# Five column sums of squares taken by TensorE as two fp32r products of the total's head and rest, two of them asked for one or two groups later

## The reference, cut to what matters

```python
h = rmsnorm(x, g_mix)
z = h @ w_in                                   # lx, lg, q, k, v
y_lru = rmsnorm(rg_lru(conv(lx)) * gelu(lg), g_lru_out)
y_att = rmsnorm(chunk_window_attention(q, k, v, sinks), g_attn_out)
x = x + concatenate([y_lru, y_att]) @ w_out
h = rmsnorm(x, g_ffn)
x = x + square(relu(h @ w_ff1)) @ w_ff2
gate = sigmoid(rmsnorm(x, g_ple) @ w_ple_gate)
x = x + gate * (p @ w_ple_proj)
return rmsnorm(x, g_final)
```

## Time and profile before

| | us |
|---|---|
| median of 3 runs | 1088.73 |
| lowest and highest of the 3 | 1082.97 and 1088.93 |
| the profiled execution, whole | 1087.07 |
| its span, first to last instruction | 1085.3 |

### The profile page before, as it was taken

The page is one execution under the profiler, slowest core; times in us unless marked ns, Lnnn a source line. Parts: engine busy times, 40 slices in busy tenths (PEclk is TensorE's granted clock), DMA queues, the critical chain, the costliest instruction groups (busy, mean ns, idle before and its releaser), DMA issues.

```text
span 1085.3 us, 13820 instructions
## 1 busy us (share of the span) xinstructions
PE 1068.8 (98%) x4930; PEld 877.6 (81%) x4930; DVE 688.1 (63%) x928; ACT 460.3 (42%) x797; POOL 423.8 (39%) x285
## 2 busy tenths in 40 slices
PE   9999999999998999999999999999999999999996
PEld 7888787777876788888888888888888888888896
DVE  7997778878699644544544544544545545697558
ACT  7446745555584322422422422422422422565334
POOL 0121151334127235445445445445445345294221
PEclk9999999999999999999999999999999999999998
DMA  8111102111011112112112112112112111420004
GB/s 330 40 40 39 39 1 88 39 40 40 1 40 39 39 39 77 39 39 77 39 39 77 39 39 77 39 39 77 39 39 76 40 39 73 160 78 1 1 1 156
DMA packets 20162, 61.05 MB, mean 56 GB/s; under 512 B 2080, under 2 KB 4128, under 8 KB 20128
## 3 DMA queue, kind: packets, MB, share of 16 engines
q1 hardware_dynamic: 19440, 59.82, 15.1%
q10 hardware_dynamic: 688, 0.79, 0.2%
HBM read 56.40 MB, written 4.19 MB: 56 GB/s over the span
## 4 chain that ended last, share of the span: by engine, by line
PE 79%; DVE 6%; ACT 2%; issue 1%; DVEq 0%; ACTq 0%
PE bank L576 25%; PE bank L577 25%; PE bank L578 25%; PE bank L683 1%; DVE xT L1781 1%; PE bank L713 1%; PE bank L698 1%; ACT raw L1129 1%; DVE h_lo L1730 1%; PE bank L641 1%; DVE t_lo L1730 1%; DVE xT L1860 1%; DVE r_fin L1362 0%; ACT h_hi L1121 0%; DVE gt L1854 0%
## 5 line engine op out<-in xcount | busy, mean ns | idle before, releaser
L576 PE MATMUL bank<-h_hi,w_hi 128*128 128x512 f32 (+1 forms) x722 | 281.2, 389 | 4.3 <-DVE h_lo L1730 3.7
L577 PE MATMUL bank<-h_lo,w_hi 128*128 128x512 f32 (+1 forms) x722 | 275.2, 381 | 0.0
L578 PE MATMUL bank<-h_hi,w_lo 128*128 128x512 f32 (+1 forms) x722 | 275.1, 381 | 0.0
L1781 DVE TENSOR_TENSOR xT<-bank,xT 128x512 f32<-128x512 f32 x256 | 172.4, 688 | 110.4 <-PE bank L578 110.4
L576 PE MATMUL bank<-u_hi,w_hi 128*128 128x512 f32 x512 | 199.5, 390 | 0.1
L578 PE MATMUL bank<-u_hi,w_lo 128*128 128x512 f32 x512 | 199.2, 389 | 0.0
L577 PE MATMUL bank<-u_lo,w_hi 128*128 128x512 f32 x512 | 199.2, 389 | 0.0
L576 PEld LDWEIGHTS bank<-h_hi,w_hi 128*128 128x128 f32 x722 | 136.1, 188 | 36.3 <-issue 5.2
L577 PEld LDWEIGHTS bank<-h_lo,w_hi 128*128 128x128 f32 x722 | 136.1, 189 | 27.2 <-issue 2.2
L578 PEld LDWEIGHTS bank<-h_hi,w_lo 128*128 128x128 f32 x722 | 136.2, 189 | 26.2
L530 POOL TENSOR_TENSOR w_lo<-w_raw,w_hi 128x1024 fp32r<-128x1024 f32 x30 | 71.9, 2419 | 121.2 <-ACT w_hi L1220 121.2
(11 more groups left out here) (225 smaller groups left out, 1715.1 us busy)
## 6 DMA issues: line engine op xcount, KB each, us to landing
w_raw<-in_w_ff SPq DMA_DIRECT2D x60, 512.0 KB, 3.6
stage<-in_w_in SPq DMA_DIRECT2D x13, 512.0 KB, 6.5
stage<-in_w_out SPq DMA_DIRECT2D x8, 512.0 KB, 4.1
stage<-in_w_ple_gate SPq DMA_DIRECT2D x8, 512.0 KB, 3.6
xT<-in_x SPq DMA_DIRECT2D x7, 512.0 KB, 10.3
stage<-in_w_ff SPq DMA_DIRECT2D x4, 512.0 KB, 3.2
out_x<-xT SPq DMA_DIRECT2D x4, 512.0 KB, 3.0
out_x<-xT SPq DMA_DIRECT2D x6, 256.0 KB, 2.2
```

The lines of the kernel that those rows point to most:

```text
L576: pe.matmul(o, whi, hh, start=first, stop=False, skip_group_check=onto)
L577: pe.matmul(o, whi, hl, start=False, stop=False, skip_group_check=onto)
L578: return pe.matmul(o, wlo, hh, start=False, stop=last, skip_group_check=onto)
L1781: dve.tensor_tensor(dst, bank[4 + q % 4][:, :], dst, ALU.add).then_inc(y_added, 1)
```

## The change

For the sums 4, 5, 6, 8 and 9 the float32 product with ones becomes two fp32r products into the same bank: one of the total's head, one of its rest. Sums 0 to 3, 7 and 10 to 12 stay as they are. The head is a new copy on ACT (`total_head`), the rest a new subtraction (`total_rest`) on POOL for sums 4, 6, 8 and 9 and on DVE for sum 5; it is written where the total stands. `ones_r` is an fp32r copy of the ones, made once on ACT early in the input projection. `sum_rows` now waits for the rest (`total_low`) instead of the last addition (`sq_used`), which `total_head` waits for. Sum 5 moves from behind A group 1 to behind A group 2, sum 6 from behind A group 9 to behind A group 11. Sums 4, 8 and 9 keep their places on PE.

```diff
@@ build
+        total_lo = at("total_lo", T + 4 * KB, [P, SEQ], F32R)
+        att_total_hi = at("att_total_hi", T + 12 * KB, [P, SEQ], F32R)
+        ffn_total_hi = at("ffn_total_hi", KV, [P, SEQ], F32R)
+        total2_lo = at("total2_lo", KV + 4 * (PAD + SEQ), [P, SEQ], F32R)
...
+        def total_rest(eng, n):
+
+            src, hi, lo = total_parts(n)
+            eng.wait_ge(total_high, SPLIT_SUMS.index(n) + 1)
+            eng.tensor_tensor(lo, src, hi, ALU.subtract).then_inc(total_low, 1)
@@ POOL
                 probs(u)
+                if u == UNITS - 3:
+                    total_rest(pool, SS_ATT)
             low(2 * 10)
             low(2 * 10 + 1)
             sums(SS_FFN, sq, acc)
+            total_rest(pool, SS_FFN)
...
             low(2 * GATE_FIRST)
             low(2 * GATE_FIRST + 1)
+            total_rest(pool, SS_PLE)
             low(2 * (GATE_FIRST + 1))
             low(2 * (GATE_FIRST + 1) + 1)
             sums(SS_PLE + 1, sq2, acc2)
+            total_rest(pool, SS_PLE + 1)
@@ PE, sum_rows
-                pe.wait_ge(sq_used, SQ_BY[n])
                 if n >= 1:
                     pe.wait_ge(rms_done, n)
                 tok, width = span(n)
-                pe.matmul(bank[b][:, 0:width], ones[:, :], total[:, tok], start=True, stop=True
-                          ).then_inc(ss_done, 1)
+                if n in SPLIT_SUMS:
+                    _, hi, lo = total_parts(n)
+                    pe.wait_ge(ones_ready, 1)
+                    pe.wait_ge(total_low, SPLIT_SUMS.index(n) + 1)
+                    pe.matmul(bank[b][:, 0:width], ones_r[:, :], hi, start=True, stop=False)
+                    pe.matmul(bank[b][:, 0:width], ones_r[:, :], lo, start=False, stop=True).then_inc(ss_done, 1)
+                else:
+                    pe.wait_ge(sq_used, SQ_BY[n])
+                    pe.matmul(bank[b][:, 0:width], ones[:, :], total[:, tok], start=True, stop=True
+                              ).then_inc(ss_done, 1)
@@ PE, A groups
-                if g == 1:
+                if g == 2:
                     sum_rows(SS_ATT + 1, acc, 5)
-                if g == 9:
+                if g == 11:
                     sum_rows(SS_FFN, acc, 7)
@@ ACT
+            def total_head(n):
+
+                src, hi, _ = total_parts(n)
+                act.wait_ge(sq_used, SQ_BY[n])
+                act.activation(hi, src, ACT.Copy).then_inc(total_high, 1)
...
                 if u + 2 < UNITS:
                     exps(u + 2)
+                if u == UNITS - 3:
+                    total_head(SS_ATT)
                 if u == 6:
                     root(SS_ATT, 4, r_mix, ATT)
...
             high(2 * 10 + 1)
+            total_head(SS_ATT + 1)
             root(SS_ATT + 1, 5, r_mix, ATT)
...
                 if k == 1:
+                    total_head(SS_FFN)
                     piece_free(act, 9)
...
             gate_high(GATE_FIRST)
+            total_head(SS_PLE)
             keep(0)
...
                 sigmoid(q)
+                if q == 0:
+                    total_head(SS_PLE + 1)
@@ DVE
             add_a(0)
             add_a(1)
+            total_rest(dve, SS_ATT + 1)
             invert(SS_ATT + 1, r_mix)
```

More of the change, by code:

```diff
@@ L81 @@
 RING_FREE = 2
+SPLIT_SUMS = (SS_ATT, SS_ATT + 1, SS_FFN, SS_PLE, SS_PLE + 1)
 PRODUCTS = 7
@@ L178, in build @@
             small[name] = at(name, at_byte, shape)
+            if name == "r_mix":
+                ple_total_hi = at("ple_total_hi", at_byte, shape, F32R)
             at_byte += -(-4 * int(np.prod(shape[1:])) // 32) * 32
@@ L181, in build @@
         relu = at("relu", KV + 2 * 4 * (PAD + SEQ), [P, 2, HALF])
+        ones_r = at("ones_r", at_byte, [P, P], F32R)
         nsink, eps, lam = (small[n] for n in ("nsink", "eps", "lam"))
@@ L201, in build @@
         out_done = [sem(f"out_done{pair}") for pair in range(KD // 2)]
+        ones_ready, total_high, total_low = sem("ones_ready"), sem("total_high"), sem("total_low")
         consts, w_split, sq_used, p_ready, pool_chain = (
@@ L251, in right, with total_parts @@
             return (h[:, 0:LT, half(1)], t[2], t[1], t[3], h[:, LT:KD, half(0)], h[:, LT:KD, half(1)], t[4])[i]
+        def total_parts(n):
+            tok = span(n)[0]
+            if n < SS_PLE:
+                return acc[:, tok], (att_total_hi if n < SS_FFN else ffn_total_hi)[:, tok], total_lo[:, tok]
+            return acc2[:, tok], ple_total_hi[:, tok], total2_lo[:, tok]
+        def total_rest(eng, n):
+            src, hi, lo = total_parts(n)
+            eng.wait_ge(total_high, SPLIT_SUMS.index(n) + 1)
+            eng.tensor_tensor(lo, src, hi, ALU.subtract).then_inc(total_low, 1)
         def unit_tile(u):
@@ L1026, in lru_gates @@
                 act.activation(lru_r[:, :], lru_r[:, :], ACT.Exp, scale=c_exp[:, j:j + 1]).then_inc(lru_exp, 1)
+            act.activation(ones_r[:, :], ones[:, :], ACT.Copy).then_inc(ones_ready, 1)
             for g in range(IN_GROUPS):
```

## The result

The changed kernel is slower by less than 1%: median 1092.47 us of 20 runs (1087.21 to 1094.36) against 1086.78 us of 20 runs of the kernel before (1081.73 to 1089.36); ratio 1.0043, 95% interval 1.0028 to 1.0058. The profiled execution took 1092.78 us, its span 1091.0 against 1085.3. The times of either kernel lie in two groups some 5 us apart (before: 8 runs from 1081.7 to 1083.1 and 12 from 1086.2 to 1089.4; changed: 7 from 1087.2 to 1087.7, one at 1089.5, 12 from 1092.0 to 1094.4). Experiments 7 to 10 show why.

A forecast was written before the change was run, and what follows sets the result against it. PE, busy 98% of the span, was taken to bound the kernel. Sum 4 +8.3, clock +0.6, sums 5 and 6 -0.8, sums 8 and 9 -0.8 gave +7.3 us: 1095.3 us, range 1088 to 1100.

The forecast's parts named there:

- The price of a product: On PE: two fp32r products take 0.46 us in place of 0.86; for sum 4 the gain is 0.39.
- Sum 4: PE waits for sum 4's rest, then for POOL's probs(6): turn_p(6) comes 8.3 us later; bound 5.0.
- the predicted first wait: On PE before sum 4: 5.4 us of waiting for the rest on POOL, until 239.15.
- The clock: PE's low clock costs nothing after the first wait, 0.6 us (0 to 1.6) after the second.
- rival that put a full low-clock stretch behind the second wait: Both waits at sum 4 are followed by the low clock: +8.3 to +9.9 us, 1096 to 1099; chance 0.20.
- Sum 5: Behind A group 2: DVE's reads end later, groups 6 and 7 wait 0.45 us, the 0.40 gained is given back.
- Sums 5 and 6 together: With both sums moved, the feed-forward loop starts 0.8 us earlier; bounds 0.35 and 1.26.
- Sums 8 and 9: PE waits for neither rest on POOL: 0.80 us gained; bound 0 if later POOL work comes back on PE.
- The sum: All terms over the whole kernel: +7.3 us, bounds +2.9 and +9.6.
- The base: Time of the kernel before: 1087.07 us profiled or 1088.73 shown median; the forecast 1095.3 lies between the two bases.
- only the first wait counts: Only PE's wait before sum 4 costs time, POOL's delayed low(18) and low(19) don't: +3.4 us, 1091; chance 0.11.
- The wait does not happen: Head and rest of sum 4 are done by 233.7, before PE asks: -2.4 us, 1084.7; chance 0.09.

The follow-up runs named there:

- Experiments 7 to 10: low(18), low(19) behind probs(6) in the kernel before, 1082.55 us; POOL waiting for DVE's h_lo in e1, kernel before, changed kernel: 1080.39, 1082.46, 1087.44 us.
- e1: Changed kernel with ACT's head of sum 4 ahead of exps(7) and POOL's rest behind probs(6): median 1085.19 us, ratio to the kernel before 0.9968.
- e3: Kernel before with sum 4 alone changed, all other sums float32 in their old places: 1096.39 us, ratio 1.0081.
- experiment 7: Kernel before with POOL's low(18) and low(19) behind probs(6) instead of ahead of it: one execution, 1082.55 us.
- e4: Changed kernel with POOL's rest of sum 4 behind probs(6), the head still behind exps(7): 1092.8 us, ratio to the kernel before 1.0044.
- e6: e1 with sum 6 as before, one float32 product behind A group 9: 1085.86 us, ratio to the kernel before 0.9983.
- e10: Changed kernel with POOL's splits of the second block's w2 piece waiting for DVE's four h_lo: 1087.44 us, ratio to the kernel before 1.0022.
- e9: Kernel before with POOL's splits of the second block's w2 piece waiting for DVE's four h_lo: 1082.46 us, ratio 0.9965.
- e8: e1 with POOL's splits of the second block's w2 piece waiting for DVE's four h_lo: 1080.39 us, ratio to the kernel before 0.9948.

## Why the prediction was right, step by step

**The price of a product** held: 0.46 for 0.86, and 0.39 less for sum 4, seen once it didn't wait (e1).

**Sum 4**, the step that set the sign, held in its mechanism: head behind `exps(7)`, POOL held from 221.35 to 237.34, two waits, no part of it given back (e3). Its size was 7.2 in place of 8.3. The term took the end of `exps(7)` from the kernel before, where POOL's splits had slowed DVE; by holding POOL the change removed that, and the head came 0.9 us sooner against PE's work (experiment 7). The other 0.2 is in POOL's shorter rows (1.26 + 4.66 + 1.86 = 7.78 against 7.94) and handovers. With the splits back in their place (e4) sum 4 starts 5.4 us late, which is the predicted first wait.

**The clock** held for the first wait: low behind it and hidden by the second. The second wait was 1.39 us, just under the 1.6 to 3.2 put for it, since POOL was done earlier. The 0.6 us for it didn't come: behind it the clock was 1.00. The rival that put a full low-clock stretch behind the second wait falls here. That rival had 8 products as the length of a stretch; the traces have 5 to 12, so 12 hidden ones (e3) left 0.34 us of the second wait, and a longer stretch would have shown.

**Sum 5** gave its 0.40 and I had it given back. The step that failed is the end of group 2's read on DVE, put 2.3 us later. DVE's four scalings ahead of it took 2.74 us instead of 3.40. All of that is in the first of them, 0.75 instead of 1.41: POOL's addition, which had run beside it at 260.19, now ran beside the reciprocal, at 268.69. That the addition held it is read from these two traces, not tested. So the read ended 1.7 us later and groups 6 and 7 didn't wait.

```profile
270.71 2.74 DVE L1642 SCALAR_TENSOR_TENSOR qT<-qT,vec,r_mix 128x512 f32<-128x512 f32 x4
273.37 0.68 DVE L1697 TENSOR_TENSOR xT<-bank,xT 128x512 f32<-128x512 f32 x1
```

**Sums 5 and 6 together** came to -1.05, between the taken -0.8 and the bound of -1.26; the part of sum 6 is shown by e6. The 0.2 that it lacks to the bound lies in no wait of PE and isn't explained. **Sums 8 and 9** came to -0.81, as taken.

**The sum** of these terms is 7.2 - 1.05 - 0.8 = +5.3 us where the text had +7.3. e10 against e9 measured +5.0. So the mechanism was right and the sum 2 us too dear: sum 4, the clock and sum 5 all erred to the same side.

**The base** was in part luck. The three runs shown had two of the upper group, and the forecast stood on 1088. The medians of 20 fell in the upper group for both kernels, 12 runs of 20 each time. Had the lower group been the larger one, the median would have been near 1087.4, below the stated range: 7 of the 20 runs are. The prediction took the 5 us between the groups as spread and had no cause for it.

**The rivals.** Of them, *only the first wait counts* fell with the strict order: POOL idled 16.00 us with ready splits behind the rest. So the first-in order that the Trainium skill (TensorE: Matmul & The Clock Gate, section Architectural detail: the array is 16x 32x32, not 1x 128x128) states is borne out for POOL too. *The wait does not happen* is e1, made by hand: -2.3 by the stages B and D, -2.1 by the times of e8 against e9. The text's -2.4 for it is near, but by a wrong sum: it counts the 0.40 of sum 6 twice, in the 1.99 and in the 0.86, and takes off the 0.45 of sum 5 that didn't come.

## What to carry to other kernels

Before splitting an operation into steps on other engines, find for each step what is queued ahead of it and behind it: here the 1.9 us of new work filled gaps, and its places in two queues cost 7 us against a possible gain of 2. Put the producer's step ahead of the long work in its queue, and the waiting step behind all work that is ready. A duration read from a trace holds only beside its neighbours; where the change moves POOL's work, DVE's times beside it move too.

## What the runs showed of the hardware

POOL and DVE delay each other by whole instructions, not by a share. A DVE instruction of 8 elements took 2.21 and 1.90 us instead of 0.17 beside POOL's splits and ended with them. DVE's four rests took 6.83 us when POOL had started 0.25 us sooner: the first two 2.88 and 2.83, each ending about 0.55 us after a split of POOL, the other two 0.68 as ever. POOL's two splits took 9.94 us instead of 5.33 when DVE had started 0.02 us sooner. In these traces the one that had started first was hardly slowed (POOL's splits 2.58 and 2.79 us, where they take 2.4 elsewhere), and the other waited. That came to 5 us of the whole time, and so to the two groups.

The Trainium skill (GPSIMD Engine Reference, section 8. Key points) has the two sharing their SBUF interfaces, with contention for DVE instructions with two SBUF inputs. The traces agree: beside the same splits DVE's instructions with one input in a PSUM bank (`prob<-bank,bias`) took 0.68 us and its reductions of one input 1.22, as with POOL idle.

PE's clock after a wait: low after waits of 3.71 to 5.31 us, for 5 to 12 products in the profiles, from the first product on (e4) or from 0.9 us behind the wait's end (changed kernel); high after waits of 1.39 and 0.74 us.
